# Out projection: stationary tiles of two token tiles interleaved word by word, loaded with a step of two

## The reference

```python
ga, gb = jnp.split(mg, 2, axis=-1)
merged = jax.nn.sigmoid(ga) * ya + jax.nn.sigmoid(gb) * yb
x = x + merged @ w_out[layer]
...
return _rmsnorm(x, final_g)
```

## Time and profile before

| | us |
|---|---|
| median of three runs | 1430.33 |
| profiled execution, own time | 1429.3 |
| its span | 1427.5 |
| TensorE busy | 1413.2 |
| VectorE busy | 1020.0 |
| ScalarE busy | 707.1 |

### The profile page before, as it was taken

How to read it: one execution, slowest core, us unless ns; L and a number is a source line. 1 busy time by engine, 2 the same in 40 slices (tenths; PEclk the granted TensorE clock), 3 DMA queues, 4 the chain that set the end, 5 groups by cost and what they waited for, 6 DMA issues and landing times.

```text
span 1427.5 us, 17881 instructions
## 1 busy us (share of the span) xinstructions
PE 1413.2 (99%) x6604; PEld 1175.1 (82%) x6604; DVE 1020.0 (71%) x1381; ACT 707.1 (50%) x894; POOL 31.5 (2%) x52
## 2 busy tenths in 40 slices
PE   8999999999999999999999999999999999999997
PEld 7888888888888888888888878888888888888886
DVE  6967898798878868677667656666676353478966
ACT  6546334544344456665666667555564222324434
POOL 0000000000000000000000000000000000000000
PEclk9999999999999999999999999999999999999999
DMA  8439576766756543222222434322242444617674
GB/s 300 145 125 316 177 263 186 236 213 212 238 184 207 184 146 83 79 82 81 81 81 82 114 106 133 84 72 66 81 140 74 151 125 152 207 45 247 197 254 172
DMA packets 182976, 218.43 MB, mean 153 GB/s; under 512 B 19456, under 2 KB 133248, under 8 KB 182272
## 3 DMA queue, kind: packets, MB, share of 16 engines
q1 hardware_dynamic: 174304, 197.64, 44.5%
q10 hardware_dynamic: 8608, 19.93, 3.6%
HBM read 195.51 MB, written 22.02 MB: 152 GB/s over the span
## 4 chain that ended last, share of the span: by engine, by line
PE 91%; DVE 3%; DMA 1%; ACT 1%; issue 1%; SPq 1%; POOL 0%; DVEq 0%; POOLq 0%; ACTq 0%
PE duo L2115 28%; PE duo L2117 28%; PE duo L2116 28%; PE duo L2168 2%; DMA start_y<-start_columns 1%; PE duo L2142 1%; PE duo L2145 1%; SPq L610 1%; ACT m_hi L886 1%; PE duo L2159 1%; PE duo L2164 1%; PE duo L2163 1%; PE duo L2160 1%; PE duo L2161 1%; PE duo L2598 0%
## 5 line engine op out<-in xcount | busy, mean ns | idle before, releaser
L1385 DVE TENSOR_TENSOR w_lo<-w_raw,w_hi 128x1024 fp32r<-128x1024 f32 (+1 forms) x116 | 135.3, 1167 | 99.3 <-ACT w_hi L781 98.7
L2115 PE MATMUL duo<-h_hi,w_hi 128*128 128x512 f32 x512 | 201.8, 394 | 0.0
L2117 PE MATMUL duo<-h_hi,w_lo 128*128 128x512 f32 x512 | 199.6, 390 | 0.0
L2116 PE MATMUL duo<-h_lo,w_hi 128*128 128x512 f32 x512 | 199.6, 390 | 0.0
L886 ACT ACTIVATE m_hi<-m_raw 128x2048 fp32r<-128x2048 f32 (+1 forms) x66 | 115.5, 1752 | 144.6 <-PE duo L2117 71.5
L781 ACT ACTIVATE w_hi<-w_raw 128x1024 fp32r<-128x1024 f32 (+1 forms) x118 | 119.2, 1011 | 124.3 <-DMA w_raw<-in_w_ob_dram 65.8
L1502 DVE TENSOR_TENSOR m_lo<-m_raw,m_hi 128x2048 fp32r<-128x2048 f32 (+3 forms) x71 | 141.9, 2001 | 26.9 <-ACT m_hi L886 26.5
L2115 PE MATMUL duo<-m_hi,h_hi 128*128 128x512 f32 x368 | 144.6, 393 | 1.6 <-DVE h_lo L1538 0.9
L2117 PE MATMUL duo<-m_hi,h_lo 128*128 128x512 f32 x368 | 143.3, 389 | 0.0
L2115 PE MATMUL duo<-m_hi,s_hi 128*128 128x512 f32 x320 | 124.5, 389 | 0.0
L2117 PE MATMUL duo<-m_hi,s_lo 128*128 128x512 f32 x320 | 124.5, 389 | 0.0
(11 more groups left out here) (322 smaller groups left out, 2991.0 us busy)
## 6 DMA issues: line engine op xcount, KB each, us to landing
m_raw<-in_w_in_dram SPq DMA_DIRECT2D x110, 512.0 KB, 4.7
w_raw<-in_w_in_dram SPq DMA_DIRECT2D x132, 256.0 KB, 3.0
o_raw<-in_w_out_dram SPq DMA_DIRECT2D x32, 512.0 KB, 5.1
spare<-in_w_in_dram SPq DMA_DIRECT2D x17, 512.0 KB, 4.6
h_raw<-in_w_in_dram SPq DMA_DIRECT2D x17, 512.0 KB, 4.9
w_raw<-in_w_oa_dram SPq DMA_DIRECT2D x32, 256.0 KB, 3.3
sig<-gates SPq DMA_DIRECT2D x8, 1024.0 KB, 6.3
w_raw<-in_w_ob_dram SPq DMA_DIRECT2D x32, 256.0 KB, 3.4
```

What stands on the lines that cost most here:

```text
L1385: dve.tensor_tensor(w_lo[:, piece.slot, 0:cols], w_raw[:, piece.slot, 0:cols], w_hi[:, piece.slot, 0:cols].bitcast(F32), ALU.subtract).the ...
L2115: pe.matmul(dst, lhs_hi, rhs_hi, start=start, stop=False)
L2116: pe.matmul(dst, lhs_hi, rhs_lo, start=False, stop=False)
L2117: return pe.matmul(dst, lhs_lo, rhs_hi, start=False, stop=stop)
```

## The change

Within each half of 256 tokens the two token tiles no longer lie one behind the other (128 words, then 128 words) but alternate word by word. `turn_merged` writes its transposes into every second word of the PSUM bank, so that all copies, splits and sums behind it keep that order unchanged, and each load of a stationary tile in the out projection reads 128 words with a step of two, over 1024 bytes. This holds for the merged gates and for the sums of their halves.

The moving weights of the out projection are moved against the stationary tiles: `o_raw` and `o_lo` by 64 bytes, the `o_hi` buffers by 64, 96, 32 and 0; the weights in the freed gate tiles stay at 0. `sig`, `o_a22`, `o_w` and `o_x` are moved with their neighbours. To make room, everything from 32 KB, 64 KB and 128 KB on is moved by 512 bytes each time, and the base is a multiple of 512 bytes. The number of instructions, waits and DMAs stays.

```diff
+BANKS, ROOM_AT, MOVED_BY = 512, (32, 64, 128), 64
+def of_pair(columns, j):
+    return columns.rearrange("p (c j) -> p j c", j=2)[:, j]
...
-        base = (nc.sbuf_base + 2 * KB - 1) // (2 * KB) * (2 * KB)
-        def at(name, kb, shape, dt=F32):
-            return nc.alloc_sbuf_tensor_at(name, shape, dt, offset=base + int(kb * KB))
+        base = (nc.sbuf_base + BANKS - 1) // BANKS * BANKS
+        def at(name, kb, shape, dt=F32, off=0):
+            room = BANKS * sum(kb >= edge for edge in ROOM_AT)
+            return nc.alloc_sbuf_tensor_at(name, shape, dt, offset=base + int(kb * KB) + room + off)
...
-        sig = at("sig", 48, [P, 2, TOK, SEQ])
+        sig = at("sig", 48, [P, 2, TOK, SEQ], off=2 * MOVED_BY)
...
-        o_raw = at("o_raw", 0, [P, OWN_RAW, 4 * SEQ])
-        o_lo = at("o_lo", 0, [P, OWN_RAW, 4 * SEQ], F32R)
+        o_raw = at("o_raw", 0, [P, OWN_RAW, 4 * SEQ], off=MOVED_BY)
+        o_lo = at("o_lo", 0, [P, OWN_RAW, 4 * SEQ], F32R, MOVED_BY)
...
-        o_hi = [at(f"o_hi{i}", kb, [P, 4 * SEQ], F32R) for i, kb in enumerate((48, 120, 112, 176))]
+        o_hi = [at(f"o_hi{i}", kb, [P, 4 * SEQ], F32R, off)
+                for i, (kb, off) in enumerate(((48, MOVED_BY), (120, MOVED_BY + 32), (112, MOVED_BY - 32), (176, 0)))]
...
+                    if place.turn:
+                        return of_pair(high[:, k, i % 2, :], j), of_pair(low[:, k, i % 2, :], j)
                     return high[:, k, i % 2, c], low[:, k, i % 2, c]
...
+                if place.turn:
+                    half = slice(t0, t0 + HALF_T)
+                    return of_pair(place.hi[:, k0 + k, half], j), of_pair(place.lo[:, k0 + k, half], j)
...
+            def merged_tile(kt, t):
+                half = slice(t // 2 * HALF_T, (t // 2 + 1) * HALF_T)
+                return of_pair(mg_hi[:, kt, half], t % 2), of_pair(mg_lo[:, kt, half], t % 2)
...
-                        last = three(bank[t][:, :], mg_hi[:, kt, q], mg_lo[:, kt, q], hi_of(st, j, j + 1),
+                        last = three(bank[t][:, :], *merged_tile(kt, t), hi_of(st, j, j + 1),
                                      lo_of(st, j, j + 1), kt == 0, kt == KT - 1)
...
-                    last = pe.transpose(turn_bank(kt)[:, t * P:(t + 1) * P], merged[:, cb % 2, t, c * P:(c + 1) * P], ident)
+                    half = slice(t // 2 * HALF_T, (t // 2 + 1) * HALF_T)
+                    last = pe.transpose(of_pair(turn_bank(kt)[:, half], t % 2), merged[:, cb % 2, t, c * P:(c + 1) * P], ident)
...
-                        last = three(bank[L_BANK[t]][:, :], mg_hi[:, kt, q], mg_lo[:, kt, q], hi_of(st, j, j + 1),
+                        last = three(bank[L_BANK[t]][:, :], *merged_tile(kt, t), hi_of(st, j, j + 1),
                                      lo_of(st, j, j + 1), kt == 0, kt == KT - 1)
```

More of the change, by code:

```diff
@@ L284, in hybrid_encoder @@
         part = at("part", 192, [P, TOK, SEQ])
-        o_raw = at("o_raw", 0, [P, OWN_RAW, 4 * SEQ])
-        o_lo = at("o_lo", 0, [P, OWN_RAW, 4 * SEQ], F32R)
+        o_raw = at("o_raw", 0, [P, OWN_RAW, 4 * SEQ], off=MOVED_BY)
+        o_lo = at("o_lo", 0, [P, OWN_RAW, 4 * SEQ], F32R, MOVED_BY)
         o_spare = at("o_spare", 128, [P, KT, SEQ])
         o_spare2 = at("o_spare2", 64, [P, KT, SEQ])
-        o_hi = [at(f"o_hi{i}", kb, [P, 4 * SEQ], F32R) for i, kb in enumerate((48, 120, 112, 176))]
+        o_hi = [at(f"o_hi{i}", kb, [P, 4 * SEQ], F32R, off)
+                for i, (kb, off) in enumerate(((48, MOVED_BY), (120, MOVED_BY + 32), (112, MOVED_BY - 32), (176, 0)))]
         o_a21 = at("o_a21", 192, [P, HALF_K, HALF_T])
-        o_a22 = at("o_a22", 56, [P, HALF_K, HALF_T])
+        o_a22 = at("o_a22", 56, [P, HALF_K, HALF_T], off=MOVED_BY)
         o_s12_raw = at("o_s12_raw", 96, [P, HALF_K, 2, HALF_T])
@@ L301, in hybrid_encoder @@
         o_u2 = at("o_u2", 196, [P, 2, SEQ])
-        o_w = at("o_w", 56, [P, 2, SEQ])
-        o_x = at("o_x", 60, [P, 2, SEQ])
+        o_w = at("o_w", 56, [P, 2, SEQ], off=MOVED_BY)
+        o_x = at("o_x", 60, [P, 2, SEQ], off=MOVED_BY)
         o_keep = at("o_keep", 200, [P, 2, SEQ])
@@ L345, in hybrid_encoder @@
         lam_in = at("lam_in", 186, [P, 6, A_DIM])
-        assert base + 206 * KB - 336 <= nc.sbuf_usable_end
+        assert base + 206 * KB + len(ROOM_AT) * BANKS - 336 <= nc.sbuf_usable_end
         ident = cst[:, 0:P]
@@ L2252, in start_columns @@
                         pe.wait_ge(y_read, TOK * 6 + t + 1)
-                    q = slice(t * P, (t + 1) * P)
                     for j in range(4):
                         kt = 4 * st.k + j
-                        last = three(bank[t][:, :], mg_hi[:, kt, q], mg_lo[:, kt, q], hi_of(st, j, j + 1),
+                        last = three(bank[t][:, :], *merged_tile(kt, t), hi_of(st, j, j + 1),
                                      lo_of(st, j, j + 1), kt == 0, kt == KT - 1)
```

## The result

| | before | after |
|---|---|---|
| median of 11 runs each, us | 1430.31 (1429.2 to 1430.91) | 1433.67 (1433.14 to 1435.08) |
| span of the profiled execution, us | 1427.5 | 1432.7 |
| TensorE busy, us | 1413.2 | 1417.3 |

The ratio is 1.0026, with an interval of 1.0017 to 1.0036: the change makes the kernel 3.4 us slower. The forecast was 5.6 us faster.

The account below looks back on a forecast made before the run. TensorE was taken as the bound; of 9.6 us of gaps, 4.1 us by the end of the third out projection pass plus 1.5 us in the last gave 1430.33 - 5.6 = 1424.7 us, range 1422.5 to 1437.5.

Parts of the forecast that it names:

- The bound: Whole kernel: TensorE, busy in 99% of the span and carrying 91% of the chain that ended last.
- The gap: Out projection: 0.0133 us a matmul beyond streaming, 9.6 us over 720, taken as a clash of load and stream reads.
- B: Rival: the 0.0133 us is the price of exchanging weights, so step and offset do nothing; 1430.3 us, chance 0.14.
- Loads with a step of two: Out projection: load walks as fast as the stream, offsets hold them apart; interval falls from 0.2267 to 0.2133 us.
- the 68 matmuls with an offset of 0: Out projection, of 720: operands in freed gate tiles and the last step's high half; expected to keep 0.2267 us.
- The upper bound: Out projection: matmul interval at most 0.240 us, a doubled gap, near the widest distance seen before.
- C: Rival: the gap goes but transposes slow by up to 0.109 us each; 1428.2 to 1431.7 us, chance 0.09.
- E: Rival: the gap stays and the transposes slow down; 1433.8 to 1437.3 us, chance 0.11.
- Transposes at nothing: 64 transposes writing every second PSUM word cost nothing extra, since loads set their pace of 0.109 us.
- Moves by 512 bytes at nothing: Tiles moved by 512 bytes a region leave the other matmuls' pace of 0.2267 us alone.
- The conversion to the end: Out projection to kernel end: 5.6 of TensorE's 9.6 us arrive, limited by VectorE and the start_y load.
- Rival D: All 720 out projection loads touch more places, 0.0133 us more each; slower, 1439.6 us, chance 0.13.

Follow-up runs that it names:

- m2: Small kernel of matmuls alone, 47 further settings: loads that read less, moving operands read in another order; quoted intervals 231.1, 229.9, 218.7 and 215.8 ns.
- m3: Small kernel of matmuls alone, 38 settings of the moving operand's reading order; plain 226.7 ns, halves in turn 215.8 ns, four quarters in turn 283.3 ns.
- e4: Kernel before, with the out projection's moving operand read in turn from its two halves and result columns put back: 1425.48 us, ratio 0.9966.
- e1: Changed kernel with all offsets at 0, the loads' step of two kept: 1434.27 us, ratio 1.0028.
- e6: Changed kernel, with the out projection's moving operand also read in turn from its two halves: 1425.76 us, ratio 0.9968.
- m4: Small kernel of matmuls alone, 28 settings: runs of words from two halves, swapped pairs, load steps 1 to 8; runs of one 215.8 ns, of two 333.
- m1: Small kernel of matmuls alone, 32 settings of load step, operand offsets and 256 columns; 226.7 to 233.6 ns in its table of steps 1 and 2.
- e2: Changed kernel with the two token tiles contiguous again, places and offsets kept: 1432.83 us, ratio 1.0019.
- e3: Kernel before with only the base and the three moves by 512 bytes: 1430.15 us, ratio 1.0001.

## Why the prediction was wrong, and where it was right

**The bound** was read rightly. TensorE sets the end, and a change of its pace by 4.1 us moved the median by 3.4 (2.4 to 5.1 by the interval).

**The gap** was read rightly as to its size. 0.0133 us a matmul is a cost that can be taken away, all but 2.5 ns of it (m2, m3, e4), and it is tied to the order of reading: B, the gap as a fixed price for exchanging weights, is refuted by m3 and e4, which exchange as many weights at 215.8 ns. (The gap is 13.3 ns at 256, 384 and 512 columns, but 15.9 and 16.6 at 448 and 480, m2, so two lengths were few to call it constant.) Behind B stood the Trainium skill (TensorE: Matmul & The Clock Gate, Step-by-step: what each phase is for): a load takes nothing from a running matmul. By e1 it isn't so for 512 columns in plain order, where the load's step alone adds 6.67 ns; with halves in turn it is for a load with a step of two (e6), and not for one with a step of four (238 ns, m4).

**The step that failed** is the one under "Loads with a step of two": "With a step of two the load walks 1024 bytes in the same time, as fast as the stream, and the offsets of 32 to 96 bytes hold the two apart." From the two speeds it made a picture of two readers that meet when one overtakes the other, and took the lower end of its bounds, 0.2133 us, for that picture. The load's speed wasn't measured either: 0.11 us is the distance between two loads' starts, while the same rows print 0.19 us for one load. It named the row that spoke against a clash growing or shrinking with the load's reading (half the load, not half the gap) and went past it. m1 shows that no distance helps, not even with the step of two at which the two speeds were to be equal; m2 that a load with one word to read doesn't either. Both parts of the change were meant to lower the gap, and each raises it: 13.3 ns to 20.0 by the step (e1), to 18.2 by the offsets (e2), to 19.5 by both. Nor do the 68 matmuls with an offset of 0 keep their 0.2267 us: with the step of two they take 0.2333 (e1), and for contiguous loads no place in m1 is better than 0.

**The upper bound,** 0.240 us, did hold: the mean is 0.2328, the longest interval in L 0.240. That the measured 1433.67 us lies inside the stated 1422.5 to 1437.5 is luck: the upper part of that range was there for C and E, and E's 1433.8 us is met almost to the digit while E's cause, slower transposes, didn't happen. Between ends so far apart the choice wanted a row of its own, and there was none in the trace.

**Transposes at nothing:** right, 1.91 us for sixteen as before. The rule of the Trainium skill named there (PSUM — Partial Sum Buffer, Specifications (TRN2)) isn't seen at the pace that the loads set, 0.109 us apart as before; C and E fall with it. **Moves by 512 bytes at nothing:** right, e3.

**The conversion to the end** couldn't be judged by the changed kernel, which gains nothing. e4 puts a gain of 10.9 ns on the same 720 matmuls and tests it. By the prediction's steps that is worth 4.9 us; 5.0 came out (3.0 to 6.9 by the interval), a nearness that is partly luck, since the traces show 3.7 us to the end of Y, as worked out, and 0.2 in L instead of 1.3. The waits at X5 and Y3 appeared where they were named and at about the size ("about 1 us each": 1.45 and 0.94), the one named at X4 hardly (0.32), `start_y` came 15.2 us after its issue as it had (issued 1375.28, next step 1390.51; in the changed kernel only 13.8), and the last wait of VectorE for TensorE went to nothing. So the steps to the end of Y are borne out, and L's share stays untested, because e4's readers cost VectorE 1.4 us there that the change doesn't have.

**Rival D,** slower by the load's cost, came nearest in what happened, though not in its time (1439.6 us). Its condition, an interval in L above 0.2267, was met, and all four passes paid, as it said. Its price was more than twice too high, 0.0133 us where 0.0061 was measured. And its mechanism, the number of touches, isn't borne out: the step costs nothing at 256, 384 and 480 columns, and a load of one word repeated, with 128 columns, has an interval of 231 ns in m2 and not one below 226.7.

**What stays open.** Why two words in turn from places 16 bytes apart or more bring the interval down, while runs of two are the worst of all runs, why 0, 256 and 512 bytes are good offsets in plain order, and why the load's step costs 6.7 ns at 512 columns and nothing at 480, isn't settled by these runs. They show the pattern, not its cause.

## What to carry to other kernels

A gap that is known only by its size says nothing on which of two operands has to change: before building a remedy on a picture of the clash, run rows of equal matmuls with one operand varied at a time, which costs one small kernel. Where float32 matmuls with their own load stand at 226.7 ns for 512 columns, read the moving operand in turn from its two halves and put the columns back where the result is read, and count what that costs the reading engine. Measure other lengths first: 256 columns behave otherwise. Account for the end separately, by the next engine's waits; that part of the prediction held up to the end of Y.

## What was not expected of the hardware

- A moving operand of 512 float32 columns read in turn from two places 16 bytes or more apart: 215.8 ns a matmul, plain order 226.7, words 8 bytes apart 226.7 (m3). Pairs 16 bytes apart that begin 4 bytes on take 267 (m4). The part that is left over the columns' own time is 2.5 ns: 384 columns take 162.5, so 0.4167 ns a column and 213.3 for 512.
- Four, eight and sixteen places in turn: 283, 487 and 435 ns; a plain step of two in the moving operand: 451 ns; runs of two words from two places: 333 ns (m2 to m4).
- In plain order with 512 columns: a load with a step of two adds 6.67 ns (none with 256, 384 and 480 columns), a moving operand off by 4 bytes 10.0, by 16 to 192 bytes 2 to 7, by 256 or 512 none (m1, m2). With two places in turn from the halves, step two and offsets of 4, 64 and 192 bytes add 0.9 ns or less (m3).
- Transposes into every second word of PSUM at the old 0.109 us apart, and VectorE's reading of PSUM with a step of two at the old 0.69 us for 128 x 512.
